# Recurrence of a 1-core kernel: value products as 64-column matmuls per head pair, half solve's copies divided between ScalarE and VectorE by direction, x transposes between its products

## The chip, the cores and the metric

The kernel runs on one core of a Trainium2 chip. The metric is the device time of one launch in microseconds (us). Five engines work side by side, each through its own list of instructions in order: TensorE (PE in the profile, its weight loads PEld), VectorE (DVE), ScalarE (ACT), GpSimd (POOL) and SyncE (SP, which here only issues DMAs). They wait for one another on semaphores. TensorE writes its results into PSUM, which has 8 banks of 512 floats on each of 128 partitions.

## The reference, cut to what matters

Two blocks follow one another: a trunk layer with windowed attention, a recurrence over the tokens in both directions and an MLP, then a block of latent attention and a linear recurrence. The change is in the trunk layer's recurrence over 8 heads of width 64, 256 context tokens first and then 1024 tokens, forwards and backwards:

```python
def wkv7_scan(S0, r, decay, kk, b, k, v, reverse, emit):
    xs = tuple(jnp.moveaxis(t, 1, 0) for t in (r, decay, kk, b, k, v))

    def step(S, inp):
        r_t, w_t, kk_t, b_t, k_t, v_t = inp
        sa = jnp.einsum('bhvk,bhk->bhv', S, -kk_t)
        S = S * w_t[:, :, None, :] + sa[..., None] * b_t[:, :, None, :] + v_t[..., None] * k_t[:, :, None, :]
        y = jnp.einsum('bhvk,bhk->bhv', S, r_t) if emit else None
        return S, y

    S, ys = lax.scan(step, S0, xs, reverse=reverse)
    return S, (jnp.moveaxis(ys, 0, 1) if emit else None)
...
    for d, rev in enumerate((False, True)):
        dec_c, b_c, k_c = dirs_c[d]
        S_ctx, yc_d = wkv7_scan(S0, r_c, dec_c, kk_c, b_c, k_c, v_c, rev, update_ctx)
        dec_l, b_l, k_l = dirs_l[d]
        _, y_d = wkv7_scan(S_ctx, r_l, dec_l, kk_l, b_l, k_l, v_l, rev, True)
        y_lat.append(y_d)
```

## The kernel before

The program is a sequence of blocks with a barrier after each. One of them is the function `recurrence` (L1820). It computes the scan in chunks of `CH` = 128 tokens: 10 steps s (`NCH`), of which the first two (`CC`) are the context, without outputs, and the last eight give outputs (`first_output` is 128 for s < 2 and 0 from s = 2 on, so a unit's result has 64 or 192 columns). All are float32. A step treats both directions d together; each direction has 8 heads, as 4 pairs q of two heads e, so there are 16 units u = 8d + 4e + q. All 10 steps are written out one after the other, and each engine has its own list; `ag`/`ag_free`, `dg`/`dg_free`, `eg`/`e_val`/`e_key` are the semaphores "result is there" and "bank has been read" of three groups of PSUM banks.

What TensorE does in one step, in this order:

- **Turns** (L2014): 8 groups of 4 transposes of values and factors into banks 2 and 3 in turn (`bank_a`), between the **couple products** (L2032), 64 matmuls of 64 rows into banks 0, 1, 4, 5; VectorE takes these out with a mask (L2274).
- **Crossed products** (L2043) and the **corners** (L2054, L2066), which fill in the inverses of a triangular matrix. `corner_in` waits for `x_ready`, the 32 small DMAs (L1966) that bring the step's diagonal inverses.
- The **half solve**. First the 16 products L2085 in four groups (d, e) in the order (0,0), (1,0), (0,1), (1,1), each into one whole bank 2 or 3, taken out by ScalarE with sign reversed (L2223, 128x512). Then for each head e 8 products L2095 of 64 rows and 64 columns (one half for each direction), taken out by ScalarE in two copies (L2230, 64x512, into `Cs`). Then for each e 8 products L2105 into banks 0, 1, 4, 5, which VectorE subtracts from the lower or upper half of `W` (L2291, four in a step).
- The **value products**: for each h of 8 two units, each of them two matmuls of 128 weight columns onto the same 192 (or 64) columns of bank 6 or 7 in turn: `W` with the factors (L2123), then `Vz`, the transposed values beside a half of zeros, with the keys (L2124). ScalarE takes out one half of the partitions (L2237), VectorE the other with an addition (L2302).
- The **state products** (L2138, for each direction 8 matmuls of 64 weight columns, outputs on partitions 0-63 and 64-127 in turn) and from s = 2 on the **outputs** (L2146, the same with 128 columns). VectorE makes the new state (L2311); ScalarE (s = 2 to 5, L2243) or VectorE (s = 6 to 9, L2320) takes out the outputs.
- From s = 2 on 8 **transposes of x** (L2155), whose copies are ScalarE's (L2250), and in steps 1 to 8 four **column sums** of `w_ada` (L2163), copied by L2257.

SyncE issues the DMAs of the step ahead: the inverses of step s wait for the last of VectorE's four subtractions of step s - 1 (`dg_free`, L2291), then comes the row block of x, then factors. GpSimd loads `w_ada` in 512 KB pieces (L1922), multiplies and folds each (L1932 to L1940), four pieces to a step, and waits before the next four until L2163 has read the last ones.

## Time and profile before

| | us |
|---|---|
| median of 3 runs | 3498.15 |
| lowest, highest | 3492.49, 3511.63 |
| the profiled execution | 3513.24 |
| its span in the profile | 3511.4 |
| the recurrence in it, from the first turn to the last x transpose's copy | 967.6 to 1403.0 |

### The profile page before, as it was taken

To read this page: it belongs to the slowest core of one execution; us is meant where nothing else is said; L and a number is where in the kernel's file an instruction comes from. 1 tells how busy PE (TensorE), PEld (TensorE's weight loads), DVE (VectorE), ACT (ScalarE), POOL (GpSimd) and SP (SyncE) were. 2 spreads that over 40 slices of the span, in tenths; PEclk is the share of its full clock that TensorE was granted. 3 is DMA by queue.
4 is the path that set the end of the run, shared out by engine and by line. 5 is a ranking of instruction groups with operands and counts; after the bars stand their busy time and mean duration, and the time that the engine had idled before them with its cause. 6 is when DMAs were issued, how large, how long until landed. Compare 5 with 4: busy or idle time off the path is not lost. (4 is left out here: it accounts for less than half of the span.)

```text
span 3511.4 us, 47020 instructions
## 1 busy us (share of the span) xinstructions
PE 3171.9 (90%) x18292; PEld 2493.9 (71%) x18292; DVE 1919.5 (55%) x2784; ACT 1167.7 (33%) x2305; POOL 1566.5 (45%) x1195
## 2 busy tenths in 40 slices
PE   5898999999789999799999999999897999899796
PEld 2666787788578888567788878887674666676574
DVE  3278754646434455777633463347314887666736
ACT  4145433223334443422211121102223664245713
POOL 1114646364234441466666666666450002555342
PEclk9989869999889999899999999999996999999888
DMA  4235545322144442542333333334434221222111
GB/s 169 77 120 150 162 131 174 100 79 85 57 121 136 133 134 62 170 125 88 93 96 96 96 90 96 96 102 117 127 109 116 61 61 58 78 83 66 42 55 72
DMA packets 524177, 358.50 MB, mean 102 GB/s; under 512 B 92481, under 2 KB 477238, under 8 KB 523958
## 3 DMA queue, kind: packets, MB, share of 16 engines
q1 hardware_dynamic: 513302, 325.09, 31.9%
q0 software_dynamic: 4608, 16.78, 1.6%
q10 hardware_dynamic: 6048, 13.63, 1.1%
q8 instruction: 147, 2.41, 0.3%
q14 instruction: 72, 0.59, 0.1%
HBM read 276.72 MB, written 78.18 MB: 101 GB/s over the span
## 5 line engine op out<-in xcount | busy, mean ns | idle before, releaser
L2438 PE MATMUL psum<-place,place 128*128 128x512 f32 x2126 | 861.2, 405 | 82.8 <-POOL place L2416 33.4
L2439 PE MATMUL psum<-place,place 128*128 128x512 f32 x2126 | 841.3, 396 | 0.0
L2440 PE MATMUL psum<-place,place 128*128 128x512 f32 x2126 | 839.6, 395 | 0.0
L2414 POOL CAST place<-place 128x1024 fp32r<-128x1024 f32 (+3 forms) x302 | 306.2, 1014 | 1097.8 <-PE psum L2440 658.1
L2416 POOL TENSOR_TENSOR place<-place,place 128x1024 fp32r<-128x1024 f32 (+3 forms) x302 | 693.7, 2297 | 24.1
L2438 PEld LDWEIGHTS psum<-place,place 128*128 128x128 f32 x2126 | 408.0, 192 | 200.9 <-POOL place L2416 51.9
L2439 PEld LDWEIGHTS psum<-place,place 128*128 128x128 f32 x2126 | 407.6, 192 | 90.1 <-issue 7.8
L2440 PEld LDWEIGHTS psum<-place,place 128*128 128x128 f32 x2126 | 407.0, 191 | 87.3
L657 PE MATMUL psum<-place,place 128*128 128x512 f32 (+1 forms) x712 | 289.2, 406 | 21.8 <-issue 10.3
L658 PE MATMUL psum<-place,place 128*128 128x512 f32 (+1 forms) x712 | 274.4, 385 | 0.0
L659 PE MATMUL psum<-place,place 128*128 128x512 f32 (+1 forms) x712 | 274.0, 385 | 0.0
L613 POOL CAST place<-place 128x1024 fp32r<-128x1024 f32 x44 | 47.9, 1089 | 456.7 <-DMA place<-in_w_in 434.1
L1129 POOL TENSOR_TENSOR solve<-solve 128x31 f32<-128x31 f32 (+15 forms) x310 | 208.3, 672 | 31.1 <-DMA solve<-blocks 8.5
L2529 DVE SCALAR_TENSOR_TENSOR place<-psum,mod,place 128x512 f32<-128x512 f32 x80 | 59.9, 749 | 251.6 <-PE psum L2440 251.6
L657 PEld LDWEIGHTS psum<-place,place 128*128 128x128 f32 x712 | 144.3, 203 | 57.2 <-issue 16.6
L1657 PE MATMUL psum<-place,place 96*128 96x512 f32 (+4 forms) x352 | 146.2, 525 | 24.3 <-DMA place<-gate 17.6
L659 PEld LDWEIGHTS psum<-place,place 128*128 128x128 f32 x712 | 143.9, 202 | 25.4
L658 PEld LDWEIGHTS psum<-place,place 128*128 128x128 f32 x712 | 144.9, 203 | 22.4 <-issue 1.5
L2482 ACT ACTIVATE place<-psum 128x512 f32<-128x512 f32 x64 | 38.3, 599 | 333.9 <-PE psum L2440 333.9
L2553 DVE TENSOR_TENSOR place<-place,place 128x512 fp32r<-128x512 f32 x64 | 115.4, 1803 | 49.2 <-ACT place L2484 49.2
L1699 DVE TENSOR_REDUCE cols<-psum 128x1 f32<-128x256 f32 (+7 forms) x160 | 99.7, 623 | 67.6 <-PE psum L1657 64.3
L677 ACT ACTIVATE place<-psum 128x512 f32<-128x512 f32 (+4 forms) x96 | 52.0, 541 | 233.9 <-PE psum L659 208.0
(327 smaller groups left out, 5369.9 us busy)
## 6 DMA issues: line engine op xcount, KB each, us to landing
place<-in_w_mlp_up SPq DMA_DIRECT2D x64, 512.0 KB, 4.0
place<-in_w_mlp_down SPq DMA_DIRECT2D x64, 512.0 KB, 3.6
place<-in_w_out SPq DMA_DIRECT2D x48, 512.0 KB, 3.6
chunked<-place SPq DMA_DIRECT2D x64, 320.0 KB, 3.6
place<-in_w_in SPq DMA_DIRECT2D x34, 512.0 KB, 5.6
solve<-in_w_ada POOLq DMA_DIRECT2D x32, 512.0 KB, 6.1
place<-in_lru_w_in SPq DMA_DIRECT2D x32, 512.0 KB, 4.0
place<-in_mla_w_in SPq DMA_DIRECT2D x30, 512.0 KB, 4.1
```

What stands on the lines that cost most here:

```text
L657: pe.matmul(ps, self.w_hi[:, j, k, :], hi, start=(k == 0), stop=False)
L658: pe.matmul(ps, self.w_hi[:, j, k, :], lo, start=False, stop=False)
L659: mm = pe.matmul(ps, self.w_lo[:, j, k, :], hi, start=False, stop=(k == end))
L1129: f(*args).then_inc(self.sstep, 1)
L1657: mm = pe.matmul(self.score_at(e)[:, a:a + w], q[:, b * P:(b + 1) * P], k[:, a:a + w], start=True, stop=True)
L1699: nc.vector.reduce_max(mx, ps[:, 0:n], AX_X).then_inc(self.maxed, 1)
L2414: nc.gpsimd.tensor_copy(hi, raw).then_inc(self.w_split, 1)
L2416: nc.gpsimd.tensor_tensor(lo, raw, hi.bitcast(F32), ALU.subtract).then_inc(self.w_split, 1)
L2438: pe.matmul(ps, self.w_hi[:, j, k, :], hi, start=(k == 0), stop=False)
L2439: pe.matmul(ps, self.w_hi[:, j, k, :], lo, start=False, stop=False)
L2440: mm = pe.matmul(ps, self.w_lo[:, j, k, :], hi, start=False, stop=(k == kt - 1))
L2553: tt(t["out_lo"], x, t["out_hi"].bitcast(F32), ALU.subtract).then_inc(self.hid, 1)
```

## The change

- **Value products.** They are made in four groups g of a direction and two head pairs. For each pair and head e the product with `W` is two matmuls of 64 weight columns, one for each half of the partitions, and the one with `Vz` is one matmul of the 64 columns that aren't zero. So a head pair takes 6 matmuls of 64 weight columns where it took 4 of 128. Groups 0 and 2 use banks 6 and 7, groups 1 and 3 banks 0 and 1, one for each head; group 0 waits for VectorE's first two subtractions, group 1 for all four. `eg` is counted up by two at the end of a group.
- **Half solve.** The results of direction 0 go to banks 2 and 3 and ScalarE, those of direction 1 to banks 0 and 1 and VectorE, with semaphores `second` and `second_free`; so two of four copies L2223 and two of four copies L2230 become VectorE's. The subtractions are in the order (0,0), (0,1), (1,0), (1,1).
- **x transposes and column sums.** The first four transposes stand between the two groups of L2105, the other four and the column sums behind the second, ahead of the value products. ScalarE's copies of them move with them.

```diff
-        return 20 * s + 2 * max(0, s - CC) + min(max(0, s - 1), ADA // QUAD) + x
+        return 16 * s + 2 * max(0, s - CC) + min(max(0, s - 1), ADA // QUAD) + x
...
+    def out_bank(g, e):
+
+        return (6, 0)[g % 2] + e
+
+    def out_units(h):
+
+        d, q, e = h // 4, 2 * (h // 2 % 2), h % 2
+        return d, e, q, unit(d, e, q)
...
+                    if m == 0 and s >= 1:
+                        pe.wait_ge(e_val, 8 * s)
+                        pe.wait_ge(e_key, 8 * s)
...
-                for g, (d, e) in enumerate(paired):
-                    b = bank_a(ag_of(s, 12 + g))
+                for d, e in paired:
+                    b = e if d else bank_a(ag_of(s, 12 + e))
...
-                    mm.then_inc(ag, 1)
-
-                for e in range(2):
-                    banks = [bank_a(ag_of(s, 16 + 2 * e + d)) for d in range(2)]
-                    pe.wait_ge(ag_free, ag_of(s, 12 + 2 * e + 1) + 1)
+                    mm.then_inc(second if d else ag, 1)
+
+                def square_in(e):
+                    banks = [bank_a(ag_of(s, 14 + e)), e]
+                    pe.wait_ge(ag_free, ag_of(s, 12 + e) + 1)
+                    pe.wait_ge(second_free, SECOND * s + e + 1)
...
-                for e in range(2):
-                    pe.wait_ge(ag_free, ag_of(s, 16 + 2 * e + 1) + 1)
+                def square_out(e):
+                    pe.wait_ge(ag_free, ag_of(s, 14 + e) + 1)
+                    pe.wait_ge(second_free, SECOND * s + 2 + e + 1)
...
-                for h in range(8):
-                    n = 8 * s + h
-                    pe.wait_ge(dg_free, DG * s + 2 + 2 * (h // 2 % 2) + h // 4 + 1)
-                    if n >= 2:
-                        pe.wait_ge(e_val, n - 1)
-                        pe.wait_ge(e_key, n - 1)
...
+                square_in(0)
+                square_in(1)
+                square_out(0)
+                if s >= CC:
+                    turn_x(0)
+                square_out(1)
+                if s >= CC:
+                    turn_x(1)
+                if ada_of(s) is not None:
+                    b = bank_a(ada_of(s))
...
+                z = first_output(s)
+                for g in range(4):
+                    d = g // 2
+                    pe.wait_ge(dg_free, DG * s + (4 if g == 0 else 6))
+                    if g >= 2:
+                        pe.wait_ge(e_val, 8 * s + 2 * g - 2)
+                        pe.wait_ge(e_key, 8 * s + 2 * g - 2)
...
-                        o = C.psum[:, 6 + n % 2, x * (CH + HD) + z:(x + 1) * (CH + HD)]
-                        pe.matmul(o, W[:, u, :], prods[:, u, 0, CH + z:WA], start=True, stop=False)
-                        mm = pe.matmul(o, Vz[:, PAIRS * d + q, e * CH:(e + 1) * CH], prods[:, u, 1, CH + z:WA],
-                                       start=False, stop=True)
-                    mm.then_inc(eg, 1)
+                        q = 2 * (g % 2) + x
+                        outs = [C.psum[:, out_bank(g, e), x * (CH + HD) + z:(x + 1) * (CH + HD)] for e in range(2)]
+                        for e in range(2):
+                            u = unit(d, e, q)
+                            for i in range(2):
+                                pe.matmul(outs[e][half(i), :], W[:, u, half(i)], prods[:, u, 0, CH + z:WA], start=True,
+                                          stop=(i == e))
+                        for e in (1, 0):
+                            mm = pe.matmul(outs[e][half(1 - e), :], Vz[:, PAIRS * d + q, HD + HD * e:2 * HD + HD * e],
+                                           prods[:, unit(d, e, q), 1, CH + z:WA], start=False, stop=True)
+                    mm.then_inc(eg, 2)
...
-                if s >= CC:
-                    pe.wait_ge(row_ready, 16 * (s - CC + 1))
-                    for x in range(2):
-                        b = bank_a(ag_of(s, 20 + x))
...
+                for e in range(2):
+                    dve.wait_ge(second, SECOND * s + e + 1)
+                    nc.vector.tensor_scalar(W[:, unit(1, e, 0):unit(1, e, 0) + 4, :], C.psum[:, e, :]
+                                            .rearrange("p (q n) -> p q n", n=CH), -1.0, None, ALU.mult)\
+                        .then_inc(second_free, 1)
+                for e in range(2):
+                    dve.wait_ge(second, SECOND * s + 2 + e + 1)
+                    nc.vector.tensor_copy(Cs[half(0), 4 * e:4 * e + 4, :], C.psum[half(0), e, :]
+                                          .rearrange("p (q n) -> p q n", n=CH)).then_inc(second_free, 1)
```

How the instructions stand on each engine, at the places that the next parts speak of. The names are tiles: 9070 the products `prods`, 9071 `E` (the value products' results), 9072 `W`, 9074 `Xt`, 9079 `Vz`, 9080 the row block of x, 9081 `Cs`, 9082 the state, 9068 the transposed x, 9069 the sum of outputs. Sizes are the columns of weights and of moving data. Line numbers of the changed kernel are its own.

TensorE in the half solve of a step with outputs, before:

```order
L2085 MATMUL psum<-place_9072,place_9074 128x128 [waits cornered_114,ag_free_100,dg_free_102]
L2085 MATMUL psum<-place_9072,place_9074 128x128 x3
L2095 MATMUL psum<-place_9072,place_9070 64x128 [waits ag_free_100]
L2095 MATMUL psum<-place_9072,place_9070 64x128 x7
L2095 MATMUL psum<-place_9072,place_9070 64x128 [waits ag_free_100]
L2095 MATMUL psum<-place_9072,place_9070 64x128 x7
L2105 MATMUL psum<-place_9081,place_9074 64x128 [waits ag_free_100]
L2105 MATMUL psum<-place_9081,place_9074 64x128 x7
L2105 MATMUL psum<-place_9081,place_9074 64x128 [waits ag_free_100]
```

and now:

```order
L2097 MATMUL psum<-place_9072,place_9074 128x128 [waits ag_free_100,cornered_114,dg_free_102]
L2097 MATMUL psum<-place_9072,place_9074 128x128 x3
L2108 MATMUL psum<-place_9072,place_9070 64x128 [waits second_free_116,ag_free_100]
L2108 MATMUL psum<-place_9072,place_9070 64x128 x7
L2108 MATMUL psum<-place_9072,place_9070 64x128 [waits second_free_116,ag_free_100]
L2108 MATMUL psum<-place_9072,place_9070 64x128 x7
L2119 MATMUL psum<-place_9081,place_9074 64x128 [waits second_free_116,ag_free_100]
L2119 MATMUL psum<-place_9081,place_9074 64x128 x7
L2129 MATMUL psum<-mats,place_9080 128x128 [waits row_ready_111,ag_free_100]
L2129 MATMUL psum<-mats,place_9080 128x128 x3
L2119 MATMUL psum<-place_9081,place_9074 64x128 [waits second_free_116,ag_free_100]
L2119 MATMUL psum<-place_9081,place_9074 64x128 x7
```

The products of L2095 and L2105 (now L2108, L2119) are the same and in the same order; each waits for the second semaphore as well, and the transposes of x (L2129) have come in.

VectorE in the same place, before:

```order
L2279 COPY place_9075<-psum 32x8x32
L2284 TENSOR_SCALAR place_9074<-psum 32x8x32 [waits dg_101]
L2284 TENSOR_SCALAR place_9074<-psum 32x8x32
L2291 TENSOR_TENSOR place_9072<-place_9072,psum 64x512 [waits dg_101] x4
L2302 TENSOR_TENSOR place_9071<-psum,place_9076 64x384 [waits eg_103] x8
```

and now:

```order
L2309 TENSOR_SCALAR place_9074<-psum 32x8x32 [waits dg_101]
L2309 TENSOR_SCALAR place_9074<-psum 32x8x32
L2315 TENSOR_SCALAR place_9072<-psum 128x512 [waits second_115] x2
L2320 COPY place_9081<-psum 64x512 [waits second_115] x2
L2325 TENSOR_TENSOR place_9072<-place_9072,psum 64x512 [waits dg_101] x4
L2335 TENSOR_TENSOR place_9071<-psum,place_9076 64x384 [waits eg_103] x8
```

Two 128x512 copies and two 64x512 copies stand ahead of the four subtractions (L2325).

TensorE at the end of the value products, before:

```order
L2123 MATMUL psum<-place_9070,place_9072 128x192
L2124 MATMUL psum<-place_9070,place_9079 128x192
L2123 MATMUL psum<-place_9070,place_9072 128x192 [waits e_key_105,e_val_104,dg_free_102]
L2124 MATMUL psum<-place_9070,place_9079 128x192
L2123 MATMUL psum<-place_9070,place_9072 128x192
L2124 MATMUL psum<-place_9070,place_9079 128x192
L2138 MATMUL psum<-place_9082,place_9071 64x64 [waits s_new_106,e_key_105,e_val_104]
L2138 MATMUL psum<-place_9082,place_9071 64x64 x7
```

and now (the last of the four groups):

```order
L2163 MATMUL psum<-place_9070,place_9072 64x192 x4
L2166 MATMUL psum<-place_9070,place_9079 64x192 x2
L2163 MATMUL psum<-place_9070,place_9072 64x192 [waits e_key_105,e_val_104,dg_free_102]
L2163 MATMUL psum<-place_9070,place_9072 64x192 x3
L2166 MATMUL psum<-place_9070,place_9079 64x192 x2
L2163 MATMUL psum<-place_9070,place_9072 64x192 x4
L2166 MATMUL psum<-place_9070,place_9079 64x192 x2
L2180 MATMUL psum<-place_9082,place_9071 64x64 [waits s_new_106,e_key_105,e_val_104]
```

The state products (L2138, now L2180) follow as before, on the same semaphores; the waits that stood at each fourth matmul stand at each twelfth.

ScalarE from the half solve to the end of step 3, before:

```order
L2202 ACTIVATE place_9072<-psum 128x4x64 [waits ag_99]
L2223 ACTIVATE place_9072<-psum 128x512 [waits ag_99] x4
L2230 ACTIVATE place_9081<-psum 64x512 [waits ag_99] x4
L2237 ACTIVATE place_9071<-psum 64x384 [waits eg_103] x8
L2243 ACTIVATE place_9069<-psum 128x4x128 [waits yp_107] x2
L2250 ACTIVATE place_9068<-psum 128x4x128 [waits ag_99] x2
L2257 ACTIVATE mod<-psum 128x4 [waits ag_99]
```

and now:

```order
L2228 ACTIVATE place_9072<-psum 128x4x64 [waits ag_99]
L2249 ACTIVATE place_9072<-psum 128x512 [waits ag_99] x2
L2255 ACTIVATE place_9081<-psum 64x512 [waits ag_99] x2
L2261 ACTIVATE place_9068<-psum 128x4x128 [waits ag_99] x2
L2268 ACTIVATE mod<-psum 128x4 [waits ag_99]
L2275 ACTIVATE place_9071<-psum 64x384 [waits eg_103] x8
L2281 ACTIVATE place_9069<-psum 128x4x128 [waits yp_107] x2
```

The copies of x (L2250, now L2261) and of the column sums stand ahead of the value products' copies.

## Rows read from the trace of the kernel before

**Rows 1.** The page's busy time and share of the span, by engine:

```profile
PE 3171.9 (90%) x18292; PEld 2493.9 (71%) x18292; DVE 1919.5 (55%) x2784; ACT 1167.7 (33%) x2305; POOL 1566.5 (45%) x1195
```

**Rows 2.** Steps 1 to 3: length, busy PE PEld DVE ACT POOL, clock, DMA share, GB/s:

```profile
1011.50:1052.50 41.00, 35.35 (x458) 32.76 (x457) 14.82 (x38) 14.44 (x34) 11.51 (x12) 0.88 0.39 105
1052.50:1095.90 43.40, 40.32 (x499) 35.73 (x499) 21.51 (x38) 18.58 (x39) 21.16 (x20) 1.00 0.51 140
1095.90:1140.20 44.30, 41.67 (x498) 36.95 (x498) 20.91 (x36) 18.58 (x39) 21.14 (x20) 0.96 0.48 132
```

**Rows 3.** Timeline of step 6's half solve (start, length, engine, line, [idle before]):

```profile
1246.13 3.87 PE L2085 MATMUL psum<-place,place 128*128 128x128 f32 x32
...
1250.04 0.60 ACT L2223 ACTIVATE place<-psum 128x512 f32<-128x512 f32 x1 [0.30 <-PE psum L2085]
...
1250.73 1.09 PE L2095 MATMUL psum<-place,place 64*64 64x128 f32 x16 [0.73 <-ACT place L2223]
1251.83 1.21 ACT L2230 ACTIVATE place<-psum 64x512 f32<-64x512 f32 x2 [1.19 <-PE psum L2095]
...
1253.13 0.76 PE L2095 MATMUL psum<-place,place 64*64 64x128 f32 x10 [1.31 <-ACT place L2230]
...
1255.48 1.09 PE L2105 MATMUL psum<-place,place 64*64 64x128 f32 x16 [0.76 <-ACT place L2230]
...
1256.51 0.59 PE L2123 MATMUL psum<-place,place 128*128 128x192 f32 x2
1256.61 1.40 DVE L2291 TENSOR_TENSOR place<-place,psum 64x512 f32<-64x512 f32 x2 [0.45 <-PE psum L2105]
```

**Rows 4.** Timeline of the same step's end, TensorE:

```profile
1267.10 0.69 PE L2138 MATMUL psum<-place,place 128*64 128x64 f32 x16
1267.62 1.05 PE L2146 MATMUL psum<-place,place 128*64 128x128 f32 x16
1268.49 0.64 PE L2138 MATMUL psum<-place,place 128*64 128x64 f32 x16
...
1269.93 1.09 PE L2155 MATMUL psum<-mats,place 128*128 128x128 f32 x8
1271.28 0.61 PE L2163 MATMUL psum<-mats,solve 128*128 128x1 f32 x4 [0.25 <-ACT place L2250]
...
1272.19 1.07 PE L2014 MATMUL psum<-mats,place 128*128 128x128 f32 x8
```

**Rows 5.** Timeline, ScalarE: the last copy of L2085's results in steps 0 and 1:

```profile
996.55 0.60 ACT L2223 ACTIVATE place<-psum 128x512 f32<-128x512 f32 x1 [0.35 <-PE psum L2085]
...
1036.67 0.60 ACT L2223 ACTIVATE place<-psum 128x512 f32<-128x512 f32 x1 [0.30 <-PE psum L2085]
```

**Rows 6.** Groups by line and shape, VectorE within the recurrence (count | busy, mean ns):

```profile
L2302 DVE TENSOR_TENSOR place<-psum,place 64x384 f32<-64x384 f32 x64 | 35.5, 555 | 42.6 <-PE psum L2124 41.8
L2291 DVE TENSOR_TENSOR place<-place,psum 64x512 f32<-64x512 f32 x40 | 27.4, 686 | 101.8 <-PE psum L2105 101.2
...
L2279 DVE COPY place<-psum 32x256 f32<-32x256 f32 x20 | 8.5, 424 | 19.2 <-PE psum L2054 19.0
```

**Rows 7.** Timeline: the loads ahead of step 1's corners, and the corners of steps 1 and 2:

```profile
1004.55 0.79 SPq L1966 DMA_DIRECT2D place<-inv_t  x2
...
1019.19 0.93 POOL L1922 DMA_DIRECT2D solve<-in_w_ada  x1 [0.30 <-POOL place L1940]
...
1019.35 0.91 SPq L1966 DMA_DIRECT2D place<-inv_t  x2
...
1025.01 1.08 PE L2054 MATMUL psum<-place,place 32*32 32x32 f32 x64 [2.85 <-DMA place<-inv_t]
...
1066.28 0.74 PE L2054 MATMUL psum<-place,place 32*32 32x32 f32 x64
```

**Rows 8.** The inverse loads (L1966, 320 of them), from issue to landing:

```profile
DMA to landing us min/median/max: 1.6/1.8/5.6
```

**Rows 9.** TensorE's busy us, clock and DMA share behind step 1's wait:

```profile
1025.00:1035.00 10.00, 9.99 (x164) 0.50 0.63 208
```

95 lines of the change are left out of this document (46 added, 49 removed).

## The prediction, made before the changed kernel had run

> **What bounds the kernel now.** I read the page's busy times first: TensorE is busy 90% of the span [rows 1]. The change touches only the recurrence, so the next view is the stretches, one for each step: TensorE is busy 40.3 of 43.4 us in step 2 and 41.7 of 44.3 in step 3, VectorE about half of that [rows 2]. So in a step with outputs TensorE's own list sets the length, and what counts is how long that list is and where it stands still. The timeline of a step shows both. In the half solve TensorE stands still three times for ScalarE's copies, 0.73, 1.31 and 0.76 us [rows 3]. The value products run without a gap from 1256.51 to 1267.10 [rows 3, 4]: 32 matmuls, 64 records, in 10.59 us. Behind the state products and outputs stand the x transposes and column sums, 1269.93 to 1272.19, 2.26 us, 0.25 of it a wait [rows 4]. The recurrence ends at a barrier and nothing of the next part starts ahead of it, so what is saved in it comes off the kernel's time. Steps 0 and 1 are bound otherwise: step 1's corners waited 2.85 us for the inverse loads [rows 7].
>
> **Value products.** 10.59 us less a start of 0.2 is 10.4 for 64 records of 192 columns, 0.1625 us each. Do two matmuls of 64 weight columns run side by side? The outputs L2146 have that form: 16 records of 128 columns take 1267.62 to 1268.49, 0.054 us each [rows 4], while L2085's 32 records of 128 columns and 128 weight columns take 3.87, 0.12 each [rows 3]. They alternate between the two halves of the partitions, as the new products do. So a head pair's 6 matmuls are three pairs side by side, 3 x 2 x 0.1625 = 0.975 us in place of 1.3. A step has 8 head pairs: 7.8 in place of 10.4, **2.6 saved**. Bounds: 15.6 with no overlap (the second rival below), 7.8 with all of it; I take 7.8 since L2146's row is the same form.
>
> Are the copies fast enough? A group lasts 1.95 us, and VectorE's two additions in it 2 x 0.555 = 1.11 [rows 6]. TensorE comes back to a bank pair after a whole group, so there is no wait. In steps 0 and 1 a group and its copies are about equally long (0.8 us each, below).
>
> What is late next: both results of the last group are told of together, at its end. Before, the last-but-one was being copied while TensorE made the last. Now the first copy ends about 0.35 (its start behind the products, which is 0.1 to 0.2 in the half solve [rows 3] and more for longer matmuls) + 0.555 = 0.9 us behind the last value product, and the outputs wait for it (e_val and e_key of 8s + 7), while only 0.2 + 0.5 us of state products stand ahead. **0.3 us added** (0 to 0.5).
>
> **Half solve.** From L2085's start, in us, before [rows 3]: products until 3.75, L2095 at 4.60, again at 7.00, second L2105 at 9.35, value products at 10.38. Now: ScalarE has only direction 0, VectorE direction 1. VectorE's copies aren't in the trace; I price a 128x512 or 64x512 one at 0.69, the subtraction of the same size, bounded below by 0.55 and above by 0.75 (a 32x256 copy takes 0.424) [rows 6]. The last group's copy begins at 3.91 (ScalarE's did) and ends at 4.6. The first 8 square products need none of it: 3.75 to 4.8. The next 8: 4.8 to 5.8. Copies of the first begin 1.10 behind their start [rows 3], end at 5.55. L2105's first half: 5.8 to 6.8. Four transposes: to 7.35. L2105's second half, whose copies ended at 6.6: to 8.4. Four transposes, half of L2155's 1.09 [rows 4]: to 8.95. Column sums, 0.8: to 9.75. There are two more switches between full-array and half-array matmuls than before, 0.1 each: 9.95. The subtractions that group 0 needs end at about 1.1 + 0.69 behind the second half's start, 9.2, so they are covered; if the copies took 0.75 they still would be. The value products begin at 9.95 in place of 10.38: **0.4 saved**, with the transposes and sums inside.
>
> The Trainium skill (TensorEngine Tiling, Key Properties) says that a change of tiling mode drains TensorE, which speaks against putting full-array transposes between half-array products. In the rows a switch costs little: the 16 records of L2146 fit in 0.87 before the next L2138. By the skill I would take a matmul's lag for each of the two, 0.17 (L2138's 0.69 less the 0.52 to the next start [rows 4]), 0.34 a step instead of 0.2; that is 1 us less saved over the kernel.
>
> **x transposes and column sums** are gone from the step's end: **2.26 saved** [rows 4]. Their load is there: SyncE issues the row of x behind the inverses, which are there by the corners, and the transposes come 10 us after those. The moved column sums release GpSimd's next four w_ada loads some 12 us earlier. That puts three of the four into the time in which SyncE issues the inverse loads, more than stood there before in these steps. The inverse loads have 24 us from their release (the last subtraction, at 10.6) to the next corners: 10.4 to the next step's first turn, 13.8 from there to the corners (1052.50 to 1066.28 [rows 2, 7]). Before, issue took 15.7 (1004.55 to 1020.26 [rows 7]) and landing 1.6 to 5.6 [rows 8], 17.3 to 21.3 together. They stay covered, with 3 us to spare.
>
> **A step with outputs** thus saves 0.4 + 2.6 - 0.3 + 2.3 = 5.0 us. Step 3 took 0.9 more than step 2, at a mean clock of 0.96 against 1.00 [rows 2], and steps 4, 5 and 9 like it: the clock fell to 1.2 GHz for a while behind the half solve's three waits. These waits are gone, so I count 5.9 for 3, 4 and 5. Step 9 has no column sums, its value products begin at 9.3 (the subtractions are last there), and its end is VectorE's in place of ScalarE's copy: 4.9. Sum for steps 2 to 9: 4 x 5.0 + 3 x 5.9 + 4.9 = **42.6 us**.
>
> **Steps 0 and 1.** L2085 ends at 996.4 and 1036.5, just ahead of the last copy [rows 5]. From that end the last subtraction comes 6.4 us later (two square products 2.1, L2105 to 4.1, its subtractions 0.2 and 3 x 0.69), group 0 at 5.1, the others from 6.4 on. A group has 24 records of 64 columns; L2138's 16 took 0.52 [rows 4], so 0.8 a group. With the last copies and L2138 the step ends 10.6 behind L2085's end. Step 0: last subtraction at 1002.8, step 1 begins at 1007.0 in place of 1011.5, TensorE is at its corners 10.7 later (1011.5 to 1025.01 less 2.85 [rows 7]), 1017.7. The loads are released at 1002.8; the late landing of before had a w_ada load issued at 1019.19, just ahead of the last inverses at 1019.35 [rows 7]. Now the last are issued at 1018.5, ahead of it: landing at 17.5, 1020.4, **4.6 earlier** than 1025.01 (1.8 earlier at 20.5). From the corners to L2085's end 11.5 as before: 1031.9; last subtraction 1038.3; column sums are covered by the subtractions; step 2 begins at 1042.5 in place of 1052.5. **10 us saved** so far. Then the loads must be there at 1042.5 + 13.8 = 1056.3, 18.0 behind their release: just so with 17.5, not with 20.5.
>
> **Sum**: 42.6 + 10.0 = 52.6 us. The profiled execution took 3513.2; that gives 3460.6. It lies 15 above the median of the runs shown, 3498.15, so the median comes to **3445.5 us** (1.5% faster).
>
> **Rivals.**
>
> *Step 2 becomes bound by its loads, and the clock falls.* As worked out, at 20.5 instead of 17.5 step 1's corners are 2.8 later and step 2's wait 2.5 us. Behind step 1's wait of 2.85 TensorE ran at 1.2 GHz for 10 us [rows 9], in which it does the work of 5. With a little of that in waits anyway I take 4.2 more: 9.5 in all, 3455. For it: a w_ada load now stands close to the end of both load series. If the dips in steps 3 to 5 and 9 stay as well, 3.7 more, 3459. Chance 0.27.
>
> *The halves don't overlap in the value products*, because both read the same columns of `prods` at once or a head's last product follows on the bank that was just written. Then 15.6 us in place of 7.8 in eight steps, +62, and +4 in steps 0 and 1: 52.6 saved becomes 14 lost, 3512, **slower than before**. It decides from 14.4 us a step on: what the other edits save is 32 us, 4.0 in each of eight steps, on top of the 10.4 of before. Against it: L2146 and L2138 overlap with different data in one bank. Chance 0.05.
>
> *The inverse loads end last in every step.* Three w_ada loads beside them in place of one; where landing passes 24 us behind release, TensorE waits, and the clock falls behind each wait: some 1 + 4.2 us in seven steps, 37 lost again: 3483. For it: DMA is busy 0.5 of a step [rows 2]. Against: in step 1, with three of them beside, it was 20.5. Chance 0.08.
>
> **How the numbers follow.** My forecast 0.57, the first rival 0.27, the others 0.05 and 0.08, anything else 0.03. The unknown copies and switches move my forecast by 4 us either way, and the runs shown spread over 19. The range 3431 to 3472 takes in the forecast and the first rival. About 0.5%, 17.5 us, is what a measurement of this kernel can tell from no change. Faster by more: forecast and first rival, and what is left, 0.87; within: the load rival at 3483 and the overlap rival in part, 0.10; slower 0.03.
>
> **What the profile of after would show.** Right: value products of 7.8 us in a step, two records starting together; from L2085 to the value products 9.9; one wait of about 0.3 ahead of the outputs; steps of 38.4 us at clock 1.00; step 2's corners without a wait. Wrong: value products over 8.5 us; waits for VectorE in the half solve; a wait for inverse loads from step 2 on, or stretches of 0.5 clock in steps 2 to 9.

## The result, and the profile of the changed kernel

The changed kernel takes 3480.1 us (median of 8 runs, 3463.26 to 3487.67) beside 3505.8 of the kernel before (8 runs, 3492.49 to 3518.91): ratio 0.9925, 95% interval 0.9899 to 0.995. Measured once more later, it was 3484.3 (10 runs) beside 3507.5 (20 runs): 0.994, interval 0.9918 to 0.9962. It is faster by 0.6 to 0.75%, where 1.5% was forecast; 3445.5 and its range, which ended at 3472, both missed.

The page of the changed kernel: TensorE's busy time, to be set beside [rows 1], and the queue that brings TensorE's instructions.

```profile
PE 3120.9 (90%) x18612; PEld 2442.7 (71%) x18612; DVE 1940.8 (56%) x2824; ACT 1145.1 (33%) x2265; POOL 1562.9 (45%) x1195
...
q8 instruction: 149, 2.44, 0.3%
```

TensorE is busy 51 us less, yet the kernel gained half of that. From the first turn to the recurrence's last instruction it was 435.4 us before and is 410.6 now: 24.8 less, against the 52.6 of the sum. The part behind the recurrence takes the same (2108.4 and 2107.1).

The two profiled executions lie 50 us apart (3513.2 and 3463.3), because the part ahead of the recurrence differs too, though nothing was changed in it: the recurrence begins at 967.6 and at 943.8, and in a second execution of the changed kernel at 970.7. The difference arises between 400 and 610 us, where the mean granted clock was 0.93 and 0.94 (400 to 500, 500 to 610) in the first execution of the changed kernel, 0.79 and 0.84 in its second and 0.77 and 0.85 in the kernel before. Two of the 14 profiles of this study have the short form. So a single time tells little here; the recurrence's length, which two executions of one kernel gave to within 2 to 4 us, tells more.

The stretches of the recurrence, one for each step, show where the other half stayed. Steps 1, 3, 4, 6 and 7 (length, busy PE PEld DVE ACT POOL, clock, DMA share, GB/s), answering to [rows 2]:

```profile
983.10:1021.50 38.40, 30.36 (x491) 27.83 (x488) 16.75 (x41) 12.24 (x31) 20.29 (x19) 0.82 0.51 138
...
1065.50:1110.30 44.80, 40.27 (x532) 34.97 (x529) 23.70 (x41) 16.32 (x35) 20.91 (x20) 0.92 0.46 129
1110.30:1148.50 38.20, 37.83 (x529) 32.61 (x528) 23.54 (x41) 16.32 (x35) 21.54 (x22) 1.00 0.55 154
...
1187.20:1231.90 44.70, 40.72 (x530) 35.57 (x529) 23.68 (x41) 15.72 (x34) 21.18 (x21) 0.92 0.48 132
1231.90:1277.00 45.10, 40.64 (x530) 35.40 (x528) 24.87 (x43) 15.14 (x33) 21.23 (x20) 0.92 0.46 129
```

There are two kinds of step. Four (4, 5, 8, 9) take 38.2 to 39.1 us at full clock. Four (2, 3, 6, 7) take 44.0 to 45.1 at a mean clock of 0.92, more than the 43.4 to 44.3 they took before the change. The instructions in them are the same. TensorE's waits in steps 2 to 9 name the difference (line, who was waited for: us in total, times, longest):

```profile
PE psum L2078 <- issue: 11.4, 3, 4.3
PE psum L2055 <- issue: 3.7, 1, 3.7
PE psum L2188 <- DVE place L2335: 2.2, 8, 0.3
PE psum L2066 <- DMA place<-inv_t: 0.4, 1, 0.4
```

The third row is the wait ahead of the outputs that was forecast, at its size (0.3 us a step), and the fourth is small. The first two are four stops among the corner products, for which the profile shows no releaser: no semaphore, no load, no engine. The timeline of TensorE in step 3, start and length, [idle before]:

```profile
1079.36 0.74 PE L2066 MATMUL psum<-place,place 32*32 32x32 f32 x64
1080.04 1.10 PE L2055 MATMUL psum<-place,place 128*128 128x64 f32 x8
1081.07 0.45 PE L2078 MATMUL psum<-place,place 32*32 32x32 f32 x32
1085.78 0.65 PE L2078 MATMUL psum<-place,place 32*32 32x32 f32 x32 [4.25 <-issue]
1086.36 1.97 PE L2055 MATMUL psum<-place,place 128*128 128x64 f32 x8
1088.12 5.08 PE L2097 MATMUL psum<-place,place 128*128 128x128 f32 x32
```

L2078 is one run of 64 matmuls from one loop; it breaks off after half of them and goes on 4.25 us later. What follows is slow: 1.97 us for a group that took 1.10, and 5.08 for L2097, which takes 3.81 in step 4. The stretches say why: clock 0.62 behind the stop, that is, mostly the 1.2 GHz level, then 1.00.

```profile
1081.50:1085.70 4.20, 0.03 (x4) 0.00 (x0) 0.00 (x0) 0.06 (x1) 0.00 (x0) 0.80 0.59 221
1085.70:1092.50 6.80, 6.72 (x68) 6.66 (x69) 1.53 (x3) 1.89 (x5) 0.00 (x0) 0.62 0.02 5
1092.50:1110.30 17.80, 17.52 (x248) 15.45 (x246) 10.79 (x19) 7.48 (x15) 9.57 (x9) 1.00 0.31 75
```

So step 3 lost 6.5 us (44.8 less 38.3): 4.25 of standing still and 2.2 at the lower clock. The four steps with a stop take 25.4 us more than four undisturbed ones of 38.3, and that is nearly all of the gain that is missing.

**Two observations led to a theory.** The first: count TensorE's instructions in order, weight loads, matmuls and semaphore instructions. From stop to stop it is 1025, 3327 and 1025, within one of 4, 13 and 4 times 256. The second: the queue "instruction" moves 16 KB at a time. The changed kernel has 38,288 instructions of TensorE and 149 such packets, the kernel before 37,704 and 147: one for 256, at 64 bytes each. In step 3 no such packet comes between 1065.44 and 1083.41. The DMA view just ahead of 1083.41 (share of the 16 engines in 40 slices, then the queues):

```profile
DMA  9999999998999999899899989989999999999998
...
q1 hardware_dynamic: 722, 1.48, 101.9%
q0 software_dynamic: 8, 0.02, 1.5%
```

That is 1079.4 to 1083.4: all 16 engines full with the kernel's own loads (the keys' and values' of the step, issued just ahead of the corners), and no instruction packet. In the next 1.3 us, 1083.3 to 1084.6, the loads run out and it comes:

```profile
DMA  9889656375461663514351133301111011118111
...
q1 hardware_dynamic: 106, 0.18, 38.7%
q8 instruction: 1, 0.02, 5.2%
```

It begins at 1083.41, takes 1.07 us, and TensorE goes on at 1085.78, 1.3 us after its end. The other three stops end 1.3 to 1.5 us after such a packet too.

**Theory:** TensorE runs out of instructions. Each block of 256 is fetched by DMA while the one before is worked off. The corner products, 272 instructions with the L2055 group between them, pass in 2.5 us (1124.06 to 1126.52 in step 4), some 109 a us where a whole step has 28; and the DMA engines are full just there, so where a block begins behind them, its packet is late. The change moved these places: a step has 1028 TensorE instructions before, 4 over four blocks, so the places hardly moved from step to step (108 to 134 behind the first corner product); now it has 1086 (32 more matmul records and 32 more weight loads in the value products, 6 semaphore instructions fewer; what is counted here are records, of which a float32 matmul has two, so the couple products are 32 matmuls and 64 records), 62 over, and the places wander through the step and meet the corner products' end (210 to 279 behind the first) in steps 2, 3, 6 and 7. **Rivals:** the w_ada loads that the change releases earlier collide with the corners; the faster half solve and step leave too little time, wherever the blocks begin.

### The profile page after: what moved, and what is told of

It reads as the page before. It is cut to its first block and busy times, and to the rows that moved or that the text cites. A ratio compares the mean times of both kernels' runs of the same rounds, so it can differ in the third digit from the quotient of the medians.

```text
span 3461.5 us, 47606 instructions
## 1 busy us (share of the span) xinstructions
PE 3120.9 (90%) x18612; PEld 2442.7 (71%) x18612; DVE 1940.8 (56%) x2824; ACT 1145.1 (33%) x2265; POOL 1562.9 (45%) x1195
## 5 line engine op out<-in xcount | busy, mean ns | idle before, releaser
L657 PE MATMUL psum<-place,place 128*128 128x512 f32 (+1 forms) x712 | 286.4, 402 | 22.9 <-issue 10.4
L658 PE MATMUL psum<-place,place 128*128 128x512 f32 (+1 forms) x712 | 271.6, 381 | 0.0
L659 PE MATMUL psum<-place,place 128*128 128x512 f32 (+1 forms) x712 | 270.9, 380 | 0.0
L658 PEld LDWEIGHTS psum<-place,place 128*128 128x128 f32 x712 | 143.1, 201 | 21.6 <-issue 1.2
L2515 ACT ACTIVATE place<-psum 128x512 f32<-128x512 f32 x64 | 38.3, 599 | 334.4 <-PE psum L2473 334.4
```

Of the source, the lines that this page charges most:

```text
L657: pe.matmul(ps, self.w_hi[:, j, k, :], hi, start=(k == 0), stop=False)
L658: pe.matmul(ps, self.w_hi[:, j, k, :], lo, start=False, stop=False)
L659: mm = pe.matmul(ps, self.w_lo[:, j, k, :], hi, start=False, stop=(k == end))
```

## Experiments

In what follows the recurrence's length is that of the profiled execution, from the first turn to the last instruction, before 435.4 and changed 410.6 us. The first four kernels were timed once each: 3474.2, 3477.1, 3480.8 and 3507.5 us, beside one 3487.7 of the kernel before. By the spread shown above these times decide nothing; the lengths and the places of the stops do.

**Without the w_ada loads.** Only the first two of them are made; the sums go on with old data.

```
                 pool.wait_ge(ada_ready ...)        -> only for m < 2
-                if m + 2 < ADA:
-                    pool.wait_ge(column, m + 1)
-                    load(m + 2)
+                pool.wait_ge(column, m + 1)
```

> The changed kernel without GpSimd's w_ada loads from the third on; it folds old data, so the modulation is not the reference's. My theory: TensorE's instruction fetches (16 KB, 256 instructions) come late at the corners because the DMA engines are full there, which the earlier w_ada loads brought about. Then no stop inside the corners, no half clock behind it in steps 2 to 9, each of them 38.2 to 38.7 us, the recurrence 22 to 28 us shorter than in the changed kernel (412). Rival, the stops come from the instruction count and the faster steps alone: the same four stops of 3 to 4 us in steps 2, 3, 6, 7. Rival, the clock falls by itself: half clock stays in four steps with no stop ahead of it.

Measured: recurrence 400.1 us. Step 7's stop is gone; those of steps 2, 3 and 6 are there with 2.27, 3.71 and 4.19 us, at the same instructions (270, 210 and 279 behind the first corner product). The w_ada loads add to the traffic but are not the cause: "no stop inside the corners" had been expected of them.

**Column sums back at the step's end.**

```
-                if ada_of(s) is not None:        (between half solve and value products)
-                    ... four column sums, ag
+                if ada_of(s) is not None:        (behind the outputs; ScalarE's copy likewise)
+                    ... four column sums, ag
```

> The changed kernel with the column sums back at the step's end, so that GpSimd's w_ada loads are released there as before. Fetch theory with the loads as the cause: the stops at the corners go or shorten, though the instruction count is the same; steps of 39 to 39.5 us (0.8 for the sums back on the path), recurrence about 395 to 400. Rival, the count decides: four stops stay, recurrence about 418.

Measured: recurrence 407.1; stops of 5.56, 3.93, 3.82 and 1.38 us in steps 2, 3, 6, 7, again at 270, 210, 279 and 218, and a short one of 0.48 in step 5. A step's number of instructions is the same, and so are the places. The moved sums are not what makes them.

**Places moved by 100 instructions.** 25 matmuls (in the trace four instructions each: two passes of a weight load and a matmul) ahead of the first wait of the recurrence.

```
+            for _ in range(25):
+                pe.matmul(C.psum[:, 0, 0:1], C.mat("ident"), C.mat("ones")[:, 0:1], start=True, stop=True)
```

> The changed kernel with 25 one-column matmuls (100 TensorE instructions) ahead of the recurrence's first wait, nothing else. In the changed kernel the stops were 1025, 3327 and 1025 TensorE instructions apart, multiples of 256, and fell where a 16 KB boundary lies 209 to 279 instructions behind the first corner matmul. Fetch theory: the shift moves the boundaries so that only step 5 has one there (242): one stop instead of four, recurrence about 392 to 394 us. Rival, the loads alone decide, whatever the alignment: four stops or so, about 412. Rival, the clock: no change in which steps fall.

Measured: recurrence 397.8. Steps 3, 6 and 7 now take 38.2 us each, and the stops are in steps 4, 5, 8 and 9 (2.22, 4.09, 1.76, 1.38). Other steps stop, with nothing changed but 25 idle matmuls ahead of the recurrence, which neither rival explains. But one stop, in step 5, had been expected, and four came: the 250 of step 9 lay inside the 210 to 279 seen before and had been passed over, and the places of steps 4 and 8 (303 and 312) lie behind the corner products, so a stop is possible somewhat beyond their end.

**Value products alone**, on the kernel before.

```
+                    for e in range(2):
+                        u = unit(d, e, q)
+                        for i in range(2):
+                            pe.matmul(outs[e][half(i), :], W[:, u, half(i)], ...)
+                    for e in (1, 0):
+                        mm = pe.matmul(outs[e][half(1 - e), :], Vz[:, PAIRS * d + q, HD + HD * e:2 * HD + HD * e], ...)
```

> The kernel before with the new value products alone; half solve, x transposes and column sums as before. Price of the value products: 7.85 us in place of 10.6 a step, less 0.3 for the outputs' wait, so 2.4 a step, steps of 41.0 at full clock. Its step has 32 matmuls more, so the boundaries wander by about 60 instructions a step. Fetch theory with the loads as they were before (a gap ahead of the corners): no or one or two stops, recurrence 410 to 418 against 436 before. Rival, the count decides: two to four stops of 4 us, 420 to 428.

Measured: recurrence 449.9, 14.5 us **longer** than before and beyond both of the expected ranges. The half solve is the slow one of before, yet TensorE stops five times, in steps 2, 3, 5, 6 and 7, at 270, 210, 341, 279 and 218:

```profile
PE psum L2078 <- issue: 15.0, 3, 6.7
...
PE psum L2137 <- DVE place L2307: 6.2, 8, 0.8
...
PE psum L2055 <- issue: 5.2, 1, 5.2
...
PE psum L2097 <- issue: 1.4, 1, 1.4
```

The second row is a cost of this kernel alone: its first group of value products waits for three of the four subtractions, whose order is the old one. The stops are 21.6 us. So the part that saves most of TensorE's array time costs more than it saves when it stands alone, and the faster half solve isn't needed for the stops.

**All of the change but the value products.**

```
-                        for e in range(2):           (four matmuls of 64 columns and two of Vz a pair)
-                            ...
+                        pe.matmul(o, W[:, u, :], prods[:, u, 0, CH + z:WA], start=True, stop=False)
+                        mm = pe.matmul(o, Vz[:, PAIRS * d + q, e * CH:(e + 1) * CH], prods[:, u, 1, CH + z:WA], ...)
```

> The changed kernel with the value products of before: 32 whole 128-row products of two matmuls each (W, then Vz), so TensorE again runs about 1028 instructions a step instead of 1086; half solve, x transposes and sums stay changed. Theory (TensorE stops where its next block of 256 instructions is fetched late, and the changed step's count moves those places into the corner products): the places no longer drift by 62 instructions a step, the stops in steps 2, 3, 6 and 7 are not there as a set of four at 2.9 to 4.3 us; if the places fall clear of the corner products, all ten steps take 40.8 to 41.2 us (38.3 plus the 2.6 us of the value products) and the recurrence some 410 us, as long as the changed kernel's 410.6 though its matmuls take 26 us more. Rival (the stops come of the faster half solve and step, whatever the count): four stops remain, steps 2, 3, 6, 7 take about 47 us and the recurrence about 436 us.

Measured: recurrence 404.3, one stop of 0.5 us, in step 2. Steps 3 and 4:

```profile
1082.60:1123.00 40.40, 40.37 (x499) 35.96 (x497) 23.59 (x41) 16.29 (x35) 20.76 (x21) 1.00 0.51 144
1123.00:1163.40 40.40, 40.37 (x499) 35.98 (x497) 23.57 (x41) 16.29 (x35) 21.68 (x21) 1.00 0.53 145
```

With 1029 instructions a step, one more than before, TensorE is busy 40.37 of 40.40 us, 2.1 a step more than the undisturbed steps of the whole change and 4 less than its disturbed ones. Measured again with more runs:

> The changed kernel with the value products of before, once more, now timed against before. Its first look had steps of 40.4 us, no stop over 0.6 us, and a recurrence of 404.3 us against 410.6 of the whole change. If the places decide: the same again, recurrence 403 to 406 us, time 3470 to 3478 us, a little under the changed kernel though its matmuls take 26 us more; ratio to before 0.989 to 0.992. Rival: it comes out at or over the changed kernel's 3480 us, and the first look was chance.

Measured: recurrence 400.5, with a stop of 2.7 us in step 1 and one of 0.3 in step 2; 3473.2 us (7 runs), ratio 0.9909, interval 0.9879 to 0.9939. Its centre lies under the whole change's 3480 to 3484, though not clear of it in the intervals.

**Keys' and values' loads behind the corner copies.** One wait on SyncE's queue.

```
                     sp.wait_ge(prod, NU * s)
+                    sp.wait_ge(dg_free, DG * (s - 1) + 2)
```

> The changed kernel, but SyncE issues the keys' and values' loads of a step only when VectorE has copied the corners out of PSUM, some 5 us later than now; nothing else is changed, the instruction places least of all. Theory A (the fetch of the instruction block is late because the 16 DMA engines are full of the kernel's own loads around the corner products): the stops shrink towards 1.4 us, the shortest seen with no load beside, steps 2, 3, 6, 7 fall from about 44.6 to 40 to 42 us, recurrence 393 to 402 us. Theory B (the fetch is late by itself at these places, loads or not): stops stay at 2.9 to 4.3 us and the recurrence stays at 408 to 412 us. If the later loads arrive too late for the half solve, steps grow by the wait that shows.

Measured: recurrence 389.5, one run of 3457.8. The stops stay at their places and shrink: 2.45, 1.51, 0.90 and 0.56 us. Step 3:

```profile
1096.01 0.74 PE L2067 MATMUL psum<-place,place 32*32 32x32 f32 x64
1096.68 1.10 PE L2056 MATMUL psum<-place,place 128*128 128x64 f32 x8
1097.72 0.45 PE L2079 MATMUL psum<-place,place 32*32 32x32 f32 x32
1099.69 0.45 PE L2079 MATMUL psum<-place,place 32*32 32x32 f32 x32 [1.51 <-issue]
```

The instruction packet begins at 1096.99, 1.0 us behind the first corner product, where it was 4.05 behind in the changed kernel (1083.41 less 1079.36), and TensorE goes on 2.70 after its start, there 2.37. The stops are shorter with less traffic beside the packet, and they stay at the same places: the traffic has a part in how late the packet is, and the place decides whether that matters. Once more, with more runs:

> The kernel with only the keys' and values' loads issued after the corner copies, once more, now timed. Its first look had a recurrence of 389.5 us against 410.6 of the changed kernel. If that is the shorter fetch and not chance: recurrence 387 to 393 us, stops under 2.5 us at the same places, the time 3455 to 3462 us, some 20 us under the changed kernel. Rival (chance of one look): stops of 3 to 4 us come back and the time is about 3480 us.

Measured: recurrence 393.2, stops of 2.95, 1.24, 1.72 and 1.11 us; 3470.5 us (6 runs, 3447.8 to 3475.7), ratio 0.9893, interval 0.9857 to 0.9929. The recurrence and the stops came again, a little larger but for one (1.24 for 1.51); the time missed what was expected by 8 us.

**Places moved out of the corner products' way.** 20 idle matmuls ahead of the recurrence, 18 in steps 5 and 8 each.

```
+            for _ in range(20):
+                pe.matmul(C.psum[:, 0, 0:1], C.mat("ident"), C.mat("ones")[:, 0:1], start=True, stop=True)
...
+                    if m == 0:
+                        for x in range({5: 18, 8: 18}.get(s, 0)):
+                            pe.matmul(C.psum[half(x % 2), 0, 0:1], C.mat("ident")[:, half(x % 2)], ...)
```

> The changed kernel with 56 matmuls of one column added (20 in front of the recurrence's first wait, 18 in front of the first couple product of steps 5 and 8; they write a PSUM region that is written over afterwards). They do no work; they only move the places at which a new block of 256 instructions begins to 65 to 190 instructions behind the first corner product in steps 2 to 9. Theory (the lost gain is late instruction fetch at these places and the half clock behind it): no stop over 1 us in steps 2 to 9, every step 38.2 to 39.3 us, recurrence 384 to 388 us, the kernel some 50 us under before and 24 us under the changed kernel: about 3455 us. Rival (the stops belong to the steps and their loads, not to the places): steps 2, 3, 6, 7 stay at about 44.6 us, recurrence 411 to 413 us, the time 3480 us or a little over.

Measured: recurrence 389.3, 3463.7 us (6 runs, 3457.4 to 3469.0), ratio 0.9875, interval 0.9844 to 0.9907, clear of the changed kernel's second measurement (0.9918 to 0.9962; its first begins at 0.9899). Added work that computes nothing made the kernel 16 to 21 us faster. Two stops remain of 0.9 and 1.2 us, just behind the corners (322 and 324), and step 2 waits 1.6 us for its inverse loads and has a stretch at the lower clock behind it.

```profile
PE psum L2194 <- DVE place L2341: 2.2, 8, 0.3
PE psum L2103 <- issue: 2.1, 2, 1.2
PE psum L2072 <- DMA place<-inv_t: 1.6, 1, 1.6
```

**The kernel before, its places moved by 136.** 34 idle matmuls in the wait ahead of the recurrence; nothing of the change is in it.

```
+            for _ in range(34):
+                pe.matmul(C.psum[:, 0, 0:1], C.mat("ident"), C.mat("ones")[:, 0:1], start=True, stop=True)
```

> The kernel before with 34 matmuls of one column (136 instructions with their weight loads) in front of TensorE's first wait of the recurrence, in idle time. They move every place at which a new block of 256 instructions begins by 136, from about +110 to +134 behind the first corner product to about -2 to +27, and the next to about +228 to +254, in the stretch where the changed kernel stops; the half solve, the value products and all waits are those of before. Theory (the stops come of the places alone): the kernel before now stops too, 1.4 to 4.3 us in most of steps 2 to 9 with a half-clock stretch behind, recurrence 450 to 485 us instead of 435, the time 15 to 50 us longer. Rival (the stops need the change's faster step): the recurrence stays at 434 to 437 us and the time within 5 us of before.

Measured: recurrence 473.4, 38 us longer than before; 3559.8 us (4 runs), ratio 1.0152, interval 1.0114 to 1.0189. Seven stops, one in each of steps 2 to 8, at 254 down to 232 instructions behind the first corner product (4 fewer each step from step 3 on), and one of 2.3 us in step 0. Its waits, and its steps 3 and 4:

```profile
PE psum L2068 <- issue: 30.3, 7, 5.1
...
1094.90:1145.80 50.90, 43.53 (x499) 38.95 (x499) 20.92 (x36) 18.56 (x39) 21.11 (x20) 0.90 0.41 115
1145.80:1194.90 49.10, 42.25 (x497) 37.65 (x498) 20.94 (x36) 18.56 (x39) 21.14 (x20) 0.93 0.43 118
```

The kernel before owed its times to where its blocks happened to begin. A shift of 136 instructions, about half a block, costs it 1.5%, and the fault needs neither the change's faster steps nor its loads.

**The changed kernel once more.**

> The changed kernel once more, word for word. Theory (stops belong to the places of the 256-instruction blocks, which are the same in every execution): stops again in steps 2, 3, 6 and 7 and in no other, each 2 to 5 us, recurrence 408 to 413 us. Rival (chance of one execution): other steps or other lengths. The time 3470 to 3485 us.

Measured: recurrence 408.2; stops of 2.11, 4.24, 3.92 and 3.90 us in steps 2, 3, 6 and 7 and in no other. Over all 14 profiles of this study steps 2 to 9 have 44 stops of TensorE over 0.25 us without a releaser, in 12 of the profiles (none in the kernel before and in the last one below); steps 0 and 1 have two more. Counted from the program's first TensorE instruction, the one that stood still is number 193 or 194 modulo 256 in all 44 (193 and 195 in the other two), and each of the 46 goes on 1.2 to 1.6 us after the end of an instruction packet.

**Both remedies together.**

> Both remedies in one kernel: the 56 matmuls of one column that move the block places, and the keys' and values' loads issued after the corner copies. With both, what each alone left should go: the 0.9 to 1.2 us of steps 4, 5, 7 and 8 of the first and the 2.45, 1.51 and 0.90 us of steps 2, 3 and 6 of the second. Steps 2 to 9 all 38.2 to 39.3 us, steps 0 and 1 as with late loads (37.9 and 34.7), recurrence 379 to 385 us, time 3447 to 3457 us. Rival (the late loads' gain is all of one kind with the pads' gain and the floor is reached by either): recurrence 388 to 390 us, as with one alone.

Measured: recurrence 382.9, no such stop. Steps 3 to 6, and the corners of step 3:

```profile
1084.30:1122.60 38.30, 38.00 (x532) 32.69 (x529) 23.69 (x41) 16.30 (x35) 20.89 (x20) 1.00 0.55 151
1122.60:1160.80 38.20, 37.89 (x530) 32.65 (x528) 23.60 (x41) 16.30 (x35) 21.54 (x22) 1.00 0.57 154
1160.80:1200.10 39.30, 38.99 (x566) 33.80 (x564) 23.55 (x41) 16.30 (x35) 21.17 (x20) 1.00 0.54 150
1200.10:1238.40 38.30, 37.99 (x532) 32.70 (x529) 23.82 (x41) 15.71 (x34) 21.25 (x21) 1.00 0.57 152
```

```profile
1098.19 0.74 PE L2073 MATMUL psum<-place,place 32*32 32x32 f32 x64
1098.86 1.10 PE L2062 MATMUL psum<-place,place 128*128 128x64 f32 x8
1099.90 0.75 PE L2085 MATMUL psum<-place,place 32*32 32x32 f32 x64
1100.58 1.10 PE L2062 MATMUL psum<-place,place 128*128 128x64 f32 x8
1101.71 3.81 PE L2104 MATMUL psum<-place,place 128*128 128x128 f32 x32
```

Steps 5 and 8 hold the idle matmuls, 1.1 us each. The time is 3461.3 us (6 runs, 3442.3 to 3471.7), ratio 0.9876, interval 0.984 to 0.9912: 1.24% under before, the best centre together with the pads alone, from which it can't be told apart; the recurrence of the profiled execution is 6.4 us shorter, a little more than the 2 to 4 us by which two executions of one kernel differed. The rival's 388 to 390 fell, but the time was 4 us over what was expected.

## Why the prediction was wrong

**Its terms for a step with outputs were right.** In an undisturbed step of the changed kernel, step 4, the half solve and the start of the value products, answering to [rows 3]:

```profile
1127.64 3.81 PE L2097 MATMUL psum<-place,place 128*128 128x128 f32 x32
...
1131.38 2.04 PE L2108 MATMUL psum<-place,place 64*64 64x128 f32 x32
...
1133.38 1.09 PE L2119 MATMUL psum<-place,place 64*64 64x128 f32 x16
...
1134.40 0.65 PE L2129 MATMUL psum<-mats,place 128*128 128x128 f32 x4
...
1137.38 0.87 PE L2163 MATMUL psum<-place,place 128*64 128x192 f32 x8
```

- Half solve with transposes and sums: 9.95 forecast, 9.74 measured (1127.64 to 1137.38), without a wait for ScalarE; the two added switches cost no more than the 0.1 each that were put in.
- Value products: 7.8 forecast, 7.85 measured (to the state products at 1145.23). The halves overlap; the second rival is out.
- The wait ahead of the outputs: 0.3 forecast, 0.3 in each of eight steps.
- The clock dips behind the half solve's waits, which were counted at 0.9 us in steps 3, 4, 5 and 9: gone, clock 1.00 in steps 4, 5, 8 and 9.
- A step: 38.4 forecast, 38.2 to 38.7 in steps 4, 5 and 8. These and step 9 saved 21.6 us together, against 21.7 in the sum.
- The whole sum, 52.6 us, is what the kernel with both remedies shows: 435.4 less 382.9 is 52.5. The agreement to 0.1 is luck: steps 0 and 1 saved 11.6 there in place of 10.0, steps 2 to 9 40.9 in place of 42.6, 2.2 of them used up by the idle matmuls.

**Steps 0 and 1** were off: 10.0 saved was forecast, 7.2 came, 7.5 in the second profile. The sum had the last inverse loads of step 1 land 17.5 us behind their release, 2.7 behind the time at which TensorE is at its corners (1020.4 and 1017.7). They were released at 979.06 and the corners began 21.9 behind that, later than both 17.5 and the rival's 20.5:

```profile
1000.98 1.08 PE L2066 MATMUL psum<-place,place 32*32 32x32 f32 x64 [7.43 <-DMA place<-inv_t]
```

That is 7.4 of waiting (7.45 in the second profile) where it was 2.85 before. Without the w_ada loads it was 3.8, with the column sums back 3.5, but with those loads in place and only the instructions moved 4.3 (by 100) and 3.7 (the pads), so the loads alone don't explain it, and the cause stays open. In the kernels with the remedies the two steps saved 11 to 12. Step 2 waited 0.4 for its loads; the first rival had 2.5 and a fall of the clock for it. Its mechanism is there at a smaller size where step 2 has no stop: moved by 100 and with the pads, step 2 waited 1.2 and 1.6 us and took 42.3 and 42.6 us at a mean clock of 0.92, beside 38.8 with both remedies and a wait of 0.5.

**The step that failed** is in what bounds the kernel: "what counts is how long that list is and where it stands still". Standing still was looked for among waits for semaphores and loads alone, and the value products' 32 more records a step were priced by their time in the array and nothing else. That they are, with their weight loads, 64 more instructions, which move the block places from step to step, was no term. Steps 2, 3, 6 and 7 were to take 38.4 and took 44.0 to 45.1: 25.4 us over an undisturbed 38.3. With the 2.8 from steps 0 and 1, where the loads' landing was the mis-sized term, that is the gap between 382.8 forecast and 410.6 measured, to 0.4 us.

The rest of the miss is the base. The forecast came down to 3498.15, the median of three runs; more runs of the same kernel put it at 3505.8 and 3507.5. That alone is 8 to 9 us, and the range had no room for both.

**A right number of a wrong rival.** The third rival gave 3483, close to what was measured, by a wait for the inverse loads in every step. That wait is not there: 0.4 us in eight steps. Its shape (waits of a few us, clock down behind each) was right, its cause wasn't: loads delay TensorE here through its instructions, not through its data. The prediction's own signs told them apart: "stretches of 0.5 clock in steps 2 to 9" appeared without "a wait for inverse loads".

Could the trace of before have told? In part. It shows the 16 KB packets of the instruction queue, one for 256 instructions, and the DMA engines full around the corners; it shows no stop, since every packet of steps 2 to 9 ended 2.0 us or more ahead of its need, where in the stops TensorE goes on 1.2 to 1.6 us after a packet's end. The risk could have been priced from below at nothing, and from above only by a guess.

How far ahead TensorE asks for a block, the traces bound. In each of the 46 stops it is packet j that ends just before TensorE goes on with its instruction 256 (j + 1) + 193, or one or two behind it (both counted from 0). Of the 2082 packets in the 14 profiles none begins while TensorE is more than 302 instructions short of that place. So no profile shows TensorE with more than little over one block in reserve when the next one begins to come. In step 6 of the kernel with late loads the last 302 instructions ahead of the stop took 3.9 us; the packet began 2.7 us after TensorE had passed the first of them (2.6 is the median over all packets of that profile), took 1.1, and TensorE went on 1.2 later: 5.1 in all, which is a stop of about 1 us with hardly any traffic in its way (0.90 measured). What stays open is what TensorE does in the 1.2 to 1.6 us behind the packet's end, and in the time before the packet begins.

## What to carry to other kernels

An idle stretch of TensorE with "issue" as its releaser, in the middle of one loop's matmuls, points to late instruction fetch when such stretches lie multiples of 256 instructions apart; moving them by a few idle matmuls in a wait is an experiment of one line that settles it. Splitting matmuls in two halves that run side by side saves array time but adds instructions (here 96 matmul records in place of 64); where small matmuls pass quickly (here 272 instructions in 2.5 us) count the instructions of a step, keep the count near a multiple of 256 or place the remainder, and keep large loads from being issued just ahead of such a burst. When two versions of such a kernel are compared, a difference of 1% can be the block places alone: time both with the places shifted before saying which edit is worth it.

## What the runs showed of the hardware

- TensorE stops for 0.3 to 6.7 us at a place fixed to one instruction modulo 256, in steps whose block packet starts late; with all 16 DMA engines full of the kernel's loads the packet began 4.05 us behind the corners' start, with those loads held back 1.0. The Trainium skill (Runtime: NRT & Kernel Launch, Instruction fetch mechanics) says that instructions come in 16 KiB blocks of 256 through a DMA queue of the sequencer's own; the packets here agree (149 of 16 KB). It also says that the cost of a block is mostly hidden; here it was hidden in the kernel before and cost the changed one 25 us, and the kernel before with shifted places 38. The same section of the Trainium skill gives TensorE room for 2048 instructions, eight blocks; no run here shows such a reserve: no packet begins more than 302 instructions ahead of the place where TensorE needs it, and each stop ends 1.2 to 1.6 us after one packet.
- The stop of 4.25 us in step 3 was followed by 6.8 us at a mean clock of 0.62, which added about half as much again (2.2 us).
- Value products in 64-column halves on both sides of the array took 7.85 us in place of 10.6, as the outputs' rows of before had suggested. The recurrence gained from them only when the block places were right: 382.9 and 389.3 us, beside 400.5 and 404.3 with the value products of before and 408.2 and 410.6 with the new ones and the places as they fell.
- With the same instructions ahead of it, the recurrence began at 943.8 in one execution and at 970.7 in another; between 400 and 500 us the mean clock was 0.93 and 0.79.
